# Output projections of two layers as seven block products, with the weight sums made by GpSimd during the retention

## The reference

```python
def first_block(x, c, positions, ...):
    cond = jax.nn.silu(c.astype(jnp.float32))
    for i in range(DEPTH):
        mod = cond @ ada_w[i] + ada_b[i]
        shift, scale, gate = jnp.split(mod[:, None, :], 3, axis=-1)
        h = (rms_norm_f32(x, norm_g[i]) * (1.0 + scale) + shift).astype(x.dtype)
        if i % N_MIXERS == 0:
            out = retention_mixer(h, positions, ret_w_in[j], ret_gn_g[j], ret_w_out[j])
        else:
            out = chunked_attention_mixer(h, att_w_in[j], ...)
        x = x + (gate * out.astype(jnp.float32)).astype(x.dtype)

...
    o = rms_norm_f32(o, gn_g.reshape(RET_HEADS, RET_V_DIM))
    o = o.reshape(B, S, RET_WIDTH) * jax.nn.silu(g.astype(jnp.float32))
    return o.astype(h.dtype) @ w_out
```

## Time and profile before

| | us |
|---|---|
| median of 3 runs (2433.29 to 2435.69) | 2435.27 |
| span of the profiled execution | 2432.2 |
| input projections of layer 0, up to the retention | to about 520 |
| retention, to the first matmul of output projection 0 | to 675.1 |
| output projection 0 | 675.1 to 853 |
| output projection 1 | 1739.1 to 1917 |

### The profile page before, as it was taken

How to read it: one execution, slowest core, us unless ns; L and a number is a source line. 1 busy time by engine, 2 the same in 40 slices (tenths; PEclk the granted TensorE clock), 3 DMA queues, 4 the chain that set the end, 5 groups by cost and what they waited for, 6 DMA issues and landing times.

```text
span 2432.2 us, 36012 instructions
## 1 busy us (share of the span) xinstructions
PE 2397.0 (99%) x13552; PEld 2050.3 (84%) x13552; DVE 1591.1 (65%) x2151; ACT 1173.4 (48%) x2308; POOL 1212.6 (50%) x883
## 2 busy tenths in 40 slices
PE   7999999999999999999999999999999999999999
PEld 6888898875578898899888889999988888888887
DVE  6966757488544286653667775777434489888863
ACT  5322223334444253322445556788534434888861
POOL 1644445431044445544455545666444546866664
PEclk9999999999999999999999999999999999999999
DMA  7454544494133344543333448665234253300034
GB/s 278 156 192 150 188 152 160 152 314 143 36 108 127 129 153 153 190 158 113 104 104 104 104 117 234 160 155 144 76 115 165 99 173 111 104 1 1 5 127 156
DMA packets 295724, 329.21 MB, mean 135 GB/s; under 512 B 88264, under 2 KB 226304, under 8 KB 293760
## 3 DMA queue, kind: packets, MB, share of 16 engines
q1 hardware_dynamic: 294080, 326.81, 41.9%
q10 hardware_dynamic: 1472, 0.10, 0.0%
HBM read 247.53 MB, written 79.33 MB: 134 GB/s over the span
## 4 chain that ended last, share of the span: by engine, by line
PE 85%; DVE 7%; ACT 3%; issue 2%; DMA 1%; POOL 1%; SPq 0%; DVEq 0%; ACTq 0%
PE ps L1239 22%; PE ps L1241 22%; PE ps L1240 22%; PE ps L1576 3%; PE ps L1747 2%; PE ps L1728 2%; PE ps L1491 2%; PE ps L1510 2%; PE ps L1562 2%; PE ps L1504 1%; DVE s_raw L2433 1%; PE ps L1259 1%; PE ps L1474 1%; PE ps L1447 1%; DVE s_lo L2420 1%
## 5 line engine op out<-in xcount | busy, mean ns | idle before, releaser
L1125 POOL TENSOR_TENSOR w_lo<-raw,w_hi 128x512 fp32r<-128x512 f32 (+1 forms) x450 | 643.4, 1438 | 798.9 <-ACT w_hi L1853 762.9
L1853 ACT ACTIVATE w_hi<-raw 128x512 fp32r<-128x512 f32 (+1 forms) x454 | 281.3, 628 | 776.2 <-PE ps L1241 628.8
L1239 PE MATMUL ps<-w_hi,s_hi 128*128 128x256 f32 (+2 forms) x832 | 262.8, 316 | 0.6 <-DVE u L2553 0.3
L1240 PE MATMUL ps<-w_lo,s_hi 128*128 128x256 f32 (+2 forms) x832 | 262.0, 315 | 0.0
L1241 PE MATMUL ps<-w_hi,s_lo 128*128 128x256 f32 (+2 forms) x832 | 262.0, 315 | 0.0
L1125 POOL TENSOR_TENSOR w_lo<-raw_wide,w_hi 128x512 fp32r<-128x512 f32 x112 | 157.1, 1412 | 149.6 <-ACT w_hi L1853 149.6
L2553 DVE TENSOR_TENSOR u<-u,ps 128x1024 f32<-128x1024 f32 (+1 forms) x96 | 116.4, 1212 | 142.4 <-PE ps L1241 138.8
L1239 PE MATMUL ps<-w_hi,a_hi 128*128 128x256 f32 (+2 forms) x624 | 197.0, 316 | 0.6 <-POOL w_lo L1125 0.6
L1240 PE MATMUL ps<-w_lo,a_hi 128*128 128x256 f32 (+2 forms) x624 | 196.6, 315 | 0.0
L1241 PE MATMUL ps<-w_hi,a_lo 128*128 128x256 f32 (+2 forms) x624 | 196.6, 315 | 0.0
L1239 PE MATMUL ps<-s_hi,w_hi 128*128 128x512 f32 x480 | 188.6, 393 | 3.2 <-DVE s_lo L2420 2.3
(11 more groups left out here) (349 smaller groups left out, 6244.2 us busy)
## 6 DMA issues: line engine op xcount, KB each, us to landing
raw<-in_w SPq DMA_DIRECT2D x158, 512.0 KB, 4.2
ada_c<-in_ada SPq DMA_DIRECT2D x14, 2304.0 KB, 10.5
blk<-u SPq DMA_DIRECT2D x46, 512.0 KB, 4.3
raw_wide<-in_w SPq DMA_DIRECT2D x32, 512.0 KB, 4.6
blk<-c SPq DMA_DIRECT2D x23, 512.0 KB, 3.3
blk<-m1s SPq DMA_DIRECT2D x23, 512.0 KB, 3.3
ada_first<-in_ada SPq DMA_DIRECT2D x12, 768.0 KB, 16.2
r_g<-blk SPq DMA_DIRECT2D x8, 1024.0 KB, 9.3
```

Of the source, the lines that this page charges most:

```text
L1125: pool.tensor_tensor(w_ring(w_lo, n), w_source(n), w_ring(w_hi, n).bitcast(F32), ALU.subtract)\
L1239: pe.matmul(out, a_hi_, b_hi_, start=first, stop=False, skip_group_check=True)
L1240: pe.matmul(out, a_hi_, b_lo_, start=False, stop=False, skip_group_check=True)
L1853: act.activation(w_ring(w_hi, n), w_source(n), ACT.Copy).then_inc(w_rounded, 1)
```

## The change

The output projections of layers 0 and 1 are made of seven products of half the depth (Winograd's form of Strassen's scheme) instead of eight such halves. Products m = 0 to 6 have eight slots each, 7 x 8 x 12 = 672 matmuls. Products 0, 1 and 4 multiply A11, A12 and S4 by plain blocks of the weight, products 2, 3, 5 and 6 multiply S2, S1, S3 and A22 by T2, T1, T3 and T4. S1 to S4 are sums of blocks of the left operand, T1 to T4 of blocks of the weight.

- **Weight sums.** For both layers, in eight rounds (four a layer), SP loads four pieces of 512 KB (`sum_load`), POOL makes four sums in place (`weight_sums`, four TENSOR_TENSOR of 128x1024, each waiting for the one before), SP stores them in the new DRAM tensor `sums` and waits until they have landed (`sum_store`), and only then loads the round after next into the same buffers. The eight rounds stand in POOL's program ahead of the first `low` of output projection 0. In SP's they stand between the loads of the retention heads. The loads of the first four pairs of weights follow round 6.
- **ACT** waits before its first `hi` of output projection 0 until all 32 stores have landed, and the four first `hi` stand at steps 22 to 25 of the retention.
- **Left operand.** `r_gate` takes the gain in: four SCALAR_TENSOR_TENSOR of 128x128 instead of one TENSOR_TENSOR of 128x512. POOL makes S3 (`operand_s3`), DVE makes S2, S1 and S4 (`q_sums`); ACT rounds and DVE subtracts for each product (`q_round`, `q_lower`).
- **Results.** ACT copies product 0 to SBUF (`m1_keep`). DVE adds it to the other products as they end (`first_tile`, `keep`), `m1_early`, `u2_early`, `u4_added` and `u4_gated` bring the parts into x, POOL adds four tiles (`third_rows`) at the start of the next layer. Products 2, 3, 4 end tile by tile, since the next one adds up in the same banks.
- **The next layer's rows** are complete after product 4. ACT takes the square sums of all four tiles at the start of product 5, and PE turns them at its slots 3 and 5.

```diff
+OUT_STEPS = 8
+OUT_BANK = (0, 4, 0, 0, 0, 4, 4)
+OUT_WEIGHTS = ((0, 0), (1, 0), "T2", "T1", (1, 1), "T3", "T4")
...
+            def sum_part(r, n):
+                l, p = T_ROUNDS[r]
+                w0 = w_rows(l, *((0, 0), (0, 1), (1, 1), (1, 0))[n], 2 * p)
+                sp.dma_start(t_parts[r % 2][n][:, :].rearrange("p (k n) -> p k n", k=2),
+                             t["w"][w0:w0 + 2].rearrange("k p n -> p k n")).then_inc(t_in[r % 2], 16)
...
+            def sum_store(r):
+                l, p = T_ROUNDS[r]
+                sp.wait_ge(p_sums, t_ready(r, 4))
+                for n, kind in enumerate(("T2", "T1", "T3", "T4")):
+                    sp.dma_start(sums[l][T_KINDS.index(kind)][2 * p:2 * p + 2].rearrange("k p n -> p k n"),
+                                 t_parts[r % 2][n][:, :].rearrange("p (k n) -> p k n", k=2)).then_inc(t_stored, 16)
+                sp.wait_ge(t_stored, 48 + 64 * (r + 1))
...
             projections(0, {10: r_first}, r_after)
+            sp.wait_ge(late_in, 48)
+            sp.wait_ge(w_used, product_end(11, 6))
+            sum_load(1)
+            for r in range(2):
+                sum_store(r)
+                sum_load(r + 2)
             for h in range(2, RH):
                 sp.wait_ge(r_sdone, NT * (h - 1))
                 r_load_qk(h)
@@
                 r_load_decay(h)
+                for r in (2, 3) if h == 2 else (4, 5):
+                    sum_store(r)
+                    sum_load(r + 2)
+            sum_store(6)
+            for p in range(4):
+                load_pair(0, p)
+            sum_store(7)
...
+            def weight_sums(r):
+                b11, b12, b22, b21 = (x[:, :] for x in t_parts[r % 2])
+                pool.wait_ge(t_in[r % 2], t_landed(r))
+                pool.tensor_tensor(b22, b22, b12, ALU.subtract).then_inc(p_sums, 1)
...
+                if n == OUT[0, 0]:
+                    for r in range(len(T_ROUNDS)):
+                        weight_sums(r)
+                    for p in range(4):
+                        operand_s3(0, p)
...
+                    if (l, slot) == (0, 0):
+                        act.wait_ge(t_stored, 48 + 64 * len(T_ROUNDS))
...
-                if 4 <= e < 8:
-                    hi(OUT[0, 0] + e - 4)
-                if 26 <= e < 26 + O_EARLY[0]:
-                    o_round_pair(0, 0, e - 26)
+                if 22 <= e < 26:
+                    hi(OUT[0, 0] + e - 22)
+                if 26 <= e < 26 + O_EARLY:
+                    q_round(0, 0, e - 26)
...
-                    if l < LAST and q == 2 and k == 5:
+                    if (m, k) == (5, 3):
                         turn_half(l + 1, 0, range(4))
-                    if l < LAST and q == 2 and k == 9:
+                    if (m, k) == (5, 5):
                         turn_half(l + 1, 0, range(4, 8))
...
+                for x in range(7 * OUT_STEPS):
+                    m, k = divmod(x, OUT_STEPS)
+                    if (m, k) == (1, 0):
+                        m1_keep(l)
+                    if (m, k) in rounded:
+                        q_round(l, *rounded[m, k])
+                    if (m, k) == (5, 0):
+                        for b in range(4):
+                            stats(l + 1, 0, b)
...
+                for m in (5, 6):
+                    for p in range(4):
+                        q_lower(l, m, p)
+                for b in range(4):
+                    link(dve.tensor_tensor(u2_kept[:, b], u2_kept[:, b], gate[:, 0:512], ALU.mult))
                 for b in range(4):
                     output_tile(l, 1, b)
-                if l < LAST:
-                    for b in range(4):
-                        normalized(l + 1, 0, b)
+                for b in range(4):
+                    normalized(l + 1, 0, b)
```

More of the change, by code:

```diff
@@ L111, in _ring @@
             slots += [("U", n) for n in range(6)]
-        for c in range(4):
+        for c in range(7 if l < 2 else 4):
             out[l, c] = len(slots)
-            slots += [("O", l, c, k) for k in range(PAIRS[l] // 2)]
+            slots += [("O", l, c, k) for k in range(OUT_STEPS)]
     return slots, product, out, up
@@ L380, in turn_bank @@
         def turn_bank(l, a, k):
+            if l and not a:
+                return k % 4
             return k - 2 if (l, a) == (0, 0) and k >= 4 else 4 + k % 4
@@ L1389, in outputs @@
                     order = [(k, b) for k in range(half)
-                             for b in range(4 if l == 2 and q == 0 and k < L_FIRST else 0, 4)]
+                             for b in range(4 if q == 0 and k < L_FIRST else 0, 4)]
                     if q == 3:
@@ new lines, in o_round_pair, with m1_keep @@
+            def o_round_pair(a, kp):
+                act.wait_ge(l_sdone, NT * (LH if a or kp >= 2 else LH - 1))
+                act.wait_ge(l_yready, 8)
+                if kp >= 2:
+                    act.wait_ge(l_gated, 2 * (4 * kp - 5) + a + 1)
+                act.activation(o_pair(l_ohi, a, kp), o_pair(l_o, a, kp), ACT.Copy).then_inc(o_round, 1)
+            def m1_keep(l):
+                act.wait_ge(w_used, out_end(l, 0))
+                for b in range(4):
+                    act.activation(m1_kept[:, b], ps[:, b], ACT.Copy).then_inc(o_m1, 1)
@@ L2086, in _, with last_outputs @@
+                product_slots(FIRST_BLOCK[l + 1], 0)
+            def last_outputs():
+                for x in range(2 * L_FIRST, 4 * OUT_STEPS):
+                    if OUT_STEPS <= x < 2 * OUT_STEPS and x % 2 == 0:
+                        o_round_pair(1, (x - OUT_STEPS) // 2)
+                    hi(OUT[LAST, 0] + x)
             act.dma_start(ident[:, :], t["ident"]).then_inc(const_in, 16)
@@ new lines, in outputs @@
+                for p in range(4):
+                    q_lower(l, 2, p)
+                for b in range(4):
+                    first_tile(l, b)
+                for p in range(4):
+                    q_lower(l, 3, p)
+                for b in range(4):
+                    keep(l, "u2", b)
+                for b in range(4):
+                    m1_early(b)
+                for p in range(4):
+                    q_lower(l, 4, p)
+                for b in range(4):
+                    keep(l, "u4", b)
```

513 lines of the change are left out of this document (338 added, 175 removed), and 5 rows, old and new, of the table rounded.

## The result

| kernel | median us (range) | ratio to before, 95% interval | profiled span |
|---|---|---|---|
| before | 2434.8 (2433.3 to 2435.7) | | 2432.2 |
| after | 2489.0 (2487.2 to 2490.1) | 1.0226, 1.0213 to 1.0238 | 2485.4 |

The changed kernel is 2.3% slower, 54 us. The forecast was 2455, slower, with 2478 as the top of its range: the sign was right, the size was not. The page shows the loss at once, against the earlier trace rows: PE has 27 us less in flight although it has 43.5 us less to do, so its gaps grew, and its share of the chain fell from 85% to 72%.

A forecast was written before the change was run, and what follows sets the result against it. PE's matmuls were taken to bound the kernel (85% of the chain). -43.5 matmuls, +43.5 rounds, +14 end of product 4 and +6 clock gave +20: span 2452, median 2455 us, range 2418 to 2478.

The forecast's parts named there:

- Matmuls, -43.5: Output projections: 96 matmuls fewer a layer at 0.227 us each, 43.5 us off PE, all on the path.
- Rounds, +43.5: Retention: SP's chain of loads and stores lands store 7 at 681, delaying ACT's first `hi` and step 24's keys, +43.5 us.
- The lead of 3.2 us that I subtracted: Retention, step 24: PE used the keys 3.2 us after they were made; taken off the 46.6 us delay.
- Contention: Retention: DVE and GpSimd slow each other where they meet, 1.07 us more for DVE's 128x1024, 0.4 for GpSimd's 128x512.
- the 15 of that forecast: Retention, steps 0 to 21: by the exclusive-lock rule some 15 us more lost, most hidden behind the wait for stores.
- Gate, nothing on the path: Retention: four DVE gate operations instead of one cost between nothing and 0.5 us a step, none on the path.
- End of product 4, +14: Output stages: PE waits for the next layer's rows after product 4, 7 us a layer, 14 in all.
- Everything else in the stages, 0: Output stages: additions, roundings, lower halves and operand sums hide in a product's 21.8 us; `third_rows` taken as 0.
- Clock, +6: PE's lower clock after three stops (step 22, two at product 5), 2 us each: +6, from 0 to 9.
- (1): Rival: retention rounds flow, store 7 lands near 650, retention loses 12, total 2422; chance 0.20 for 2410 to 2430.
- (2): Rival: GpSimd and DVE, or slower DMA, stretch the rounds to the upper bound, +12, 2467 to 2480; chance 0.14.
- an upper bound of 55: Retention: 2 us more for each of 8 rounds beside a busy DVE, plus slower DVE steps before, +55.

The follow-up runs named there:

- e7: Changed kernel with GpSimd's weight sums one column wide, every transfer kept (computes something else): 2484.5 us.
- e9: Changed kernel with loads of heads 2 and 3 ahead of the first and third store, ScalarE's first four roundings at steps 28 to 31: 2464.4 us.
- e4: Changed kernel without the weight sums' loads, sums and stores, T1 to T4 read from a plain block (computes something else): 2434.5 us.
- e3: Changed kernel with the retention gate one VectorE operation on 512 elements again, the gain multiplied in by ScalarE: 2487.2 us.
- e5: Changed kernel with the next layer's first half turned two weight steps later, VectorE's gates of u2 behind the turning: 2480.4 us.
- e12: On top of e4 and e5, the output stages' extra row operations made one column wide (computes something else): 2403.7 us.
- e1: Changed kernel with head 2's keys, queries and values loaded ahead of the first store of weight sums: 2490.3 us.
- e2: Changed kernel with ScalarE's first four weight roundings after retention steps 28 to 31 instead of 22 to 25: 2478.9 us.

## Why the prediction was right or wrong

- **Matmuls, -43.5: right.** The page counts 192 less, at the same pace.
- **Rounds, +43.5: the mechanism was right, the size 12.7 short.** Step by step: `r_k` of head 2 issued at 576.4 (forecast 574), landed by 584.5 (582); head 3's issued at 618.1 (614), landed by 630.2 (621); `r_q` at 630.2 (626). But for that last landing, SP's steps up to the loads at 646 are right within about 5 us. The last store landed at 690.6, not 681: 9.6 us. Of these 5.2 were there when load 6 landed, 3.2 came with the sums of round 6 (13.2 us instead of 10, beside a busy VectorE), the rest behind. But e7, with hardly any arithmetic, still lands that store at 688.7, so the mis-sized term is the landings and not the sums.
- **The lead of 3.2 us that I subtracted** was spent nearly as said: PE goes on 53.7 us late, not 56.2, 2.5 less. Then the low clock behind the stop takes 2.2 back. Timelines of PE, after (its row at 691.84 is shown above) and then before:

```profile
696.42 1.02 PE L1691 MATMUL ps<-r_v,r_s 128*128 128x512 f32 x2
```

```profile
638.10 0.38 PE L1470 MATMUL ps<-ident,r_k 128*128 128x128 f32 x2
...
640.48 1.02 PE L1504 MATMUL ps<-r_v,r_s 128*128 128x512 f32 x2
```

The granted clock is 0.50 in 691 to 696. This is the stop of step 22 in the forecast's row on the clock, priced at 2.
- **Contention: in the wrong row of the sum.** I priced it as a term of the chain. e7 shows 28.7 us of VectorE's time lost beside GpSimd and 2.4 us of retention, no more than two executions differ by. The Trainium skill, page "SBUF — State Buffer", section "SBUF: two separate sides", calls the port pair "an exclusive lock". The trace agrees: `r_tmp` takes 3.34 us at 584.55 beside a sum of GpSimd, 1.2 alone, so it waits about one sum of 2.3 us, the rule's size and not the 1.07 that I took from the trace. The 28.7 us are more than the 15 of that forecast; that most of it is hidden holds in this kernel; in e9 11 us of PE's stops stand at it. The `r_decay` operations, 7.6 us longer ahead of head 3's rotation, are not in the forecast.
- **Gate, nothing on the path: right** (e4: 0.6 us; e3: 2.1).
- **End of product 4, +14: the wait was right (7.96 and 7.60 against 7 a layer), the account of it was not.** I took it as a local wait that costs what it lasts. e5 removes it and gets 5 us back.
- **Everything else in the stages, 0: wrong, and the largest error.** With the matmuls, the end of product 4 and two of the three stops of the clock, the kernel behind the retention was to be 25.5 us shorter (-43.5 + 14 + 4); it is 3.0 shorter. That is 22.5 of the 33 us between forecast and measurement. I set each operation beside 21.8 us of a product and found room for each. Behind product 5 VectorE has u4's sums and gates, u2's sums, four splits and two weight sums, 26 us, before the rows of product 6 that open the next layer. The added work was costed by piece and never added up over the stretch that ends with the rows on which the next layer waits. With GpSimd's S3 among layer 1's weights (3.7 us of waits, put at nothing as well), 40.5 of 43.5 us are gone where the forecast had 14 and some clock. e12 shows the price: with that row work one column wide some 25 us come back.
- **Clock, +6: about right** where seen: the turning behind a stop takes 1.6 to 1.8 us more.
- **Rivals.** (1), rounds that flow, fell with the last store at 690.6. (2), the stretched rounds, is what the retention did (56.2 against an upper bound of 55), though not by dearer arithmetic, as e7 shows; its bound was added up wrongly (43.5 and eight times 2 are 59.5), and its price left out the stages. The test of the forecast by its own marks came out: the wait of over 20 us for `r_k`, the `hi` behind the last store, the two waits for `xn`. The first output matmul at 731 instead of 719 and stages of 166 and 172 us instead of 159 are the two misses.

## What to carry to other kernels

Add up the work that a change gives an engine over the whole stretch up to the row that the next stage waits for, not product by product; an engine that is 65% busy on average can have 25 us too much at the one place that counts. Bulk transfers that one queue issues landing by landing set a time of their own: first find what in any engine's order waits for their end and put that last, since until then a stop removed earlier comes back there (e7), and check where a moved transfer makes the next one late (e1 alone 0, e2 alone 10 us, both with head 3's loads moved too 25). Ask again after each change of order what contention costs: in the changed kernel taking it away gained nothing (e7), in e9 it stands in most of PE's stops that are left. A scheme that saves a share of the matmuls must be priced with its sums free first (e4), which here would have ended the matter.

## What the runs showed of the hardware

- A GpSimd sum of 128x1024 float32 takes 2.34 us alone and up to 4.61 beside VectorE; VectorE's 128x1024 takes 1.21 alone and 3.34 beside it. Three of its `r_decay` operations, of 128 columns or only one, took 0.16 to 0.29 alone and 2.1 to 2.4 beside a sum. Its operations with one operand in PSUM (`r_gate`, 112 of them) took 321 to 350 ns each, whether GpSimd ran or not.
- One core's queues moved 280 GB/s as a mean over 140 us of loads and stores, with eight slices of 3.5 us at 391 to 408; the Trainium skill, page "DMA: Bandwidth & Descriptors", section "Specifications", gives about 358 as a core's HBM limit, half of what a stack gives to two cores; these slices pass it. A group of 2 MB of stores landed 8.2 to 15.9 us after its issue, the longer times with loads of a head or a round ahead of it.
- Behind the stop of 8 us the granted clock was 0.50 (857 to 860), and behind the one of 11.6 us too (691 to 696). 16 turning matmuls took 3.5 to 3.7 us behind the stops of 8 us and 1.91 at full clock.
